# The first attention of a two-block layer rebuilt: one table set, the mask as an identity product, sums from a split softplus

## The chip, the core and the metric

The kernel runs on one core of one Trainium2 chip. A core has five engines with instruction streams of their own: TensorE (matrix products, PE in the profile, its weight loads PEld), VectorE (DVE), ScalarE (ACT), GpSimd (POOL) and SyncE (SP, which issues the transfers here). They share the memory SBUF; TensorE writes its results to PSUM, 8 banks of 128 x 512 fp32. They wait for each other by semaphores. The metric is the device time of one execution in microseconds.

## What is computed

Two blocks work on a sequence of 512 tokens and 1024 channels. The first has stick-breaking attention beside a state-space scan, the second RWKV-7, a sparse attention and two feed-forward parts. All is fp32. The change concerns the stick-breaking attention alone, 16 heads of 64 channels:

```python
z = einsum("bqhd,bkhd->bhqk", q, k) * scale
mask = s_idx < t_idx                                  # key before query
log_beta = log_sigmoid(z)
log_one_minus = where(mask, log_sigmoid(-z), 0.0)
tail = cumsum(log_one_minus, axis=3, reverse=True) - log_one_minus
weights = exp(where(mask, log_beta + tail, -inf))
out = einsum("bhqk,bkhd->bqhd", weights, v)
```

With softplus(z) = log(1 + exp(z)) the exponent is z minus the sum of softplus(z) over the keys from s up to t.

## The kernel before

The program is a chain of stages with a barrier between them; in each stage every engine has its own list of instructions, written out by hand, and the semaphores order them. No scheduler moves anything. The attention stage comes after the projections of q, k and v and ahead of a normalization (norm_sb). No transfer is issued in it: the weights of the next stages are already in a ring in SBUF.

One head is handled at a time, keys on the 128 partitions, queries along the columns. Of the 4 x 4 blocks of 128 x 128 only the 10 on and over the diagonal are kept: key block i has 512, 384, 256 and 128 columns, 1280 together, in three banks. There are two such areas in PSUM: zb (the scores) and wb (the exponent). For a head, before:

- TensorE makes the scores into zb (`scores`, L564).
- VectorE clamps them to 80 (L608) into SBUF; ScalarE takes exp (L631) and ln(1 + ...) (L633); VectorE takes the maximum with the scores in zb (L612). That is softplus. GpSimd multiplies the diagonal blocks by a mask (L650).
- TensorE makes the scores once more into wb (L588) and adds the sums over softplus with two constant matrices (L591), 10 matmuls in fp32.
- VectorE clamps wb to 0 and adds the constant `late`, which hides later keys (L620); ScalarE takes exp (L639); TensorE multiplies with v (`products`, L573), two heads into one bank; ScalarE copies each finished bank out (L627).

exp and ln lie in different table sets of ScalarE in this program, so a table load stands before each change. TensorE's order in turn hh is: sums(hh), scores of head hh + 2, products(hh - 1).

Of the kernel before, what the change touches and what calls it, by code (L numbers as in the profile page):

```python
# [13 lines left out]
P = 128  # L14
T = 512
D = 1024
KT = D // P
NB = T // P
HD = 64
H = D // HD  # L20
# [15 lines left out]
SB_W = [T - P * i for i in range(NB)]  # L36
SB_AT = [0, 512, 1024, 896]
SB_N = 1280
# [61 lines left out]
def program(nc, A, out, stop=None, dump=None):  # L100
    f32 = mybir.dt.float32
    ALU = mybir.AluOpType
    ACT = mybir.ActivationFunctionType
# [9 lines left out]
    def sem(name):  # L113

        section.append(nc.alloc_semaphore(name))
        return section[-1]
# [7 lines left out]
    with ctx:  # L124
        F = [sb(f"act{i}", [P, KT, T]) for i in range(5)]
# [10 lines left out]
        def give_up(first):  # L136

            while above and above[-1][0] >= first:
                above.pop()[1].close()

        def open_above(key, name, shape, dtype):
            one = ExitStack()
            above.append((key, one))
            return one.enter_context(nc.sbuf_tensor(name, shape, dtype))

        def restore(name):

            give_up(9)
            for i in range(5 + len(above), 9):
                F[i:] = [open_above(i, f"{name}_act{i}", [P, KT, T], f32)]  # L150
# [8 lines left out]
        late = sb("late", [P, SB_N])  # L159
        aux = sb("aux", [P, 3584])  # L160
# [6 lines left out]
        def mat(name):  # L167
            return squares[:, MAT_AT[name] * P:MAT_AT[name] * P + P]
# [307 lines left out]
        with nc.Block() as block:  # L476
            @block.scalar
            def _(act):
                nc.scalar.activation(small[:, 0:8], cols[:, COL_AT["c"]:COL_AT["c"] + 8], ACT.Silu).then_inc(c_ready, 1)  # L479
# [62 lines left out]
        checkpoint("v", v[:, :, :])  # L542


        o = F[5]
        work = F[6][:, :, :].rearrange("p a b -> p (a b)")
        clamped = [work[:, 0:SB_N], work[:, SB_N:2 * SB_N]]
        sp_m = [F[7][:, :, :].rearrange("p a b -> p (a b)")[:, i * SB_N:(i + 1) * SB_N] for i in range(2)]
        wts = [F[8][:, :, :].rearrange("p a b -> p (a b)")[:, i * SB_N:(i + 1) * SB_N] for i in range(2)]
        zb = PS[:, 0:3, :].rearrange("p a b -> p (a b)")  # L550
        wb = PS[:, 3:6, :].rearrange("p a b -> p (a b)")
        z_ready, z_taken, sp_step = sem("z_ready"), sem("z_taken"), sem("softplus_step")
        clamp_ready, log_ready, sp_ready = sem("clamp_ready"), sem("log_ready"), sem("sp_ready")
        w_ready, w_clamped, wts_ready = sem("w_ready"), sem("w_clamped"), sem("wts_ready")
        o_ready, o_taken, exp_done, late_masked = sem("o_ready"), sem("o_taken"), sem("sb_exp_done"), sem("sp_masked")
        with nc.Block() as block:
            def head(t, hh, a, b):
                return t[hh % 2 * HD:(hh % 2 + 1) * HD, hh // 2, a:b]

            @block.tensor  # L560
            def _(pe):
                def scores(hh, dst, stop):
                    for i in range(NB):
                        mm = nc.tensor.matmul(dst[:, SB_AT[i]:SB_AT[i] + SB_W[i]], head(k_, hh, i * P, (i + 1) * P),  # L564
                                              head(q, hh, i * P, T), start=True, stop=stop)
                    return mm

                def products(hh):
                    pe.wait_ge(wts_ready, hh + 1)
                    if hh >= 4 and hh % 2 == 0:  # L570
                        pe.wait_ge(o_taken, (hh - 4) // 2 + 1)
                    for i in range(NB):
                        mm = nc.tensor.matmul(PS[hh % 2 * HD:(hh % 2 + 1) * HD, 6 + hh // 2 % 2, i * P:T],  # L573
                                              v_tok[:, i, hh * HD:(hh + 1) * HD], wts[hh % 2][:, SB_AT[i]:SB_AT[i] + SB_W[i]],
                                              start=i == 0, stop=i == NB - 1)
                    mm.then_inc(o_ready, 1)


                scores(0, zb, True).then_inc(z_ready, 1)
                pe.wait_ge(sp_ready, 1)  # L580
                scores(1, zb, True).then_inc(z_ready, 1)
                for hh in range(H):
                    pe.wait_ge(late_masked, hh + 1)
                    if hh >= 1:
                        pe.wait_ge(w_clamped, hh)
                    for i in range(NB):

                        nc.tensor.matmul(wb[:, SB_AT[i]:SB_AT[i] + SB_W[i]], head(k_, hh, i * P, (i + 1) * P),  # L588
                                         head(q, hh, i * P, T), start=True, stop=False)
                        for j in range(i, NB):  # L590
                            mm = nc.tensor.matmul(wb[:, SB_AT[i] + (j - i) * P:SB_AT[i] + SB_W[i]],  # L591
                                                  mat("neg_ge" if i == j else "neg_ones"),
                                                  sp_m[hh % 2][:, SB_AT[j]:SB_AT[j] + SB_W[j]], start=False, stop=j == NB - 1)
                    mm.then_inc(w_ready, 1)
                    if hh + 2 < H:
                        pe.wait_ge(sp_ready, hh + 2)
                        scores(hh + 2, zb, True).then_inc(z_ready, 1)
                    if hh >= 1:
                        products(hh - 1)
                products(H - 1)  # L600

            @block.vector
            def _(dve):
                def softplus(hh):
                    dve.wait_ge(z_ready, hh + 1)
                    if hh >= 2:
                        dve.wait_ge(sp_ready, hh - 1)
                    nc.vector.tensor_scalar(clamped[hh % 2], zb[:, 0:SB_N], 80.0, None, ALU.min).then_inc(clamp_ready, 1)  # L608
                    dve.wait_ge(log_ready, hh + 1)
                    if hh >= 2:  # L610
                        dve.wait_ge(w_ready, hh - 1)
                    nc.vector.tensor_tensor(sp_m[hh % 2], clamped[hh % 2], zb[:, 0:SB_N], ALU.max).then_inc(sp_ready, 1)  # L612
                softplus(0)
                for hh in range(H):
                    if hh + 1 < H:
                        softplus(hh + 1)
                    dve.wait_ge(w_ready, hh + 1)
                    if hh >= 2:
                        dve.wait_ge(o_ready, hh - 1)
                    nc.vector.scalar_tensor_tensor(out=wts[hh % 2], in0=wb[:, 0:SB_N], scalar=0.0, in1=late[:, :],  # L620
                                                   op0=ALU.min, op1=ALU.add).then_inc(w_clamped, 1)

            @block.scalar
            def _(act):
                def out_pair(p):
                    act.wait_ge(o_ready, 2 * p + 2)
                    nc.scalar.copy(o[:, p, :], PS[:, 6 + p % 2, :]).then_inc(o_taken, 1)  # L627

                def logs(hh):
                    act.wait_ge(clamp_ready, hh + 1)  # L630
                    nc.scalar.activation(clamped[hh % 2], clamped[hh % 2], ACT.Exp).then_inc(exp_done, 1)  # L631
                    act.wait_ge(exp_done, hh + 1)
                    nc.scalar.activation(clamped[hh % 2], clamped[hh % 2], ACT.Ln, bias=1.0).then_inc(log_ready, 1)  # L633
                logs(0)
                for hh in range(H):
                    if hh + 1 < H:
                        logs(hh + 1)
                    act.wait_ge(w_clamped, hh + 1)
                    nc.scalar.activation(wts[hh % 2], wts[hh % 2], ACT.Exp).then_inc(wts_ready, 1)  # L639
                    if hh % 2 == 0 and hh >= 2:  # L640
                        out_pair(hh // 2 - 1)
                out_pair(H // 2 - 1)

            @block.gpsimd
            def _(pool):
                for hh in range(H):
                    pool.wait_ge(sp_ready, hh + 1)
                    for a, n in ((0, 1), (512, 1), (896, 2)):
                        part = sp_m[hh % 2][:, a:a + n * P].rearrange("p (n c) -> p n c", c=P)
                        last = nc.gpsimd.tensor_tensor(part, part, mat("lt").unsqueeze(1).to_broadcast([P, n, P]), ALU.mult)  # L650
                    last.then_inc(late_masked, 1)
        checkpoint("o", o[:, :, :])

        def conv_program(name, n_tiles, rhs, taps, w_col, b_col, dst, pair_out=None, split=None):
# [1079 lines left out]
```

## Time and profile before

| | |
|---|---|
| median of 3 runs | 3232.93 us (3232.72 to 3234.16) |
| span of the profiled execution | 3230.6 us (the profile gives no other time of it) |
| TensorE busy in the span | 2798.7 us, 87% |
| attention stage | 287.5 to 501.0 us, 213.5 us |
| busy in it: TensorE, ScalarE, VectorE, GpSimd | 205.28, 107.25, 71.51, 24.75 us |

The span is from the first to the last instruction. The stage's busy times come from the view that adds up the busy time of each engine in a stretch. Times in the timelines count from the start of the span. In them a row can stand for several instructions of one engine and line ("x8"): an fp32 matmul is recorded as two, one for each pass. Matmuls overlap at their ends, so the time from the start of one row to the start of the next is the better measure of their cost.

### The profile page before, as it was taken

To read this page: it belongs to the slowest core of one execution; us is meant where nothing else is said; L and a number is where in the kernel's file an instruction comes from. 1 tells how busy PE (TensorE), PEld (TensorE's weight loads), DVE (VectorE), ACT (ScalarE), POOL (GpSimd) and SP (SyncE) were. 2 spreads that over 40 slices of the span, in tenths; PEclk is the share of its full clock that TensorE was granted. 3 is DMA by queue.
4 is the path that set the end of the run, shared out by engine and by line. 5 is a ranking of instruction groups with operands and counts; after the bars stand their busy time and mean duration, and the time that the engine had idled before them with its cause. 6 is when DMAs were issued, how large, how long until landed. Compare 5 with 4: busy or idle time off the path is not lost. (4 is left out here: it accounts for less than half of the span.)

```text
span 3230.6 us, 31387 instructions
## 1 busy us (share of the span) xinstructions
PE 2798.7 (87%) x13080; PEld 2116.0 (65%) x13080; DVE 1350.8 (42%) x1997; ACT 736.1 (23%) x1043; POOL 84.9 (3%) x100
## 2 busy tenths in 40 slices
PE   7899999878988862999999698999986398899997
PEld 7777555666446722888888356887852155688786
DVE  0221331565114337554444335665312733466633
ACT  0232551223003321000000113222212144322222
POOL 0000110000000000001000000000000000000000
PEclk9999998978888975999899698999977699899998
DMA  5221001201112200000000011322203000122221
GB/s 198 76 85 46 1 1 39 69 25 46 52 59 68 82 17 0 1 1 1 1 1 1 10 61 50 98 95 87 92 10 116 0 1 5 48 98 98 92 92 39
DMA packets 45244, 158.57 MB, mean 49 GB/s; under 512 B 5056, under 2 KB 6976, under 8 KB 44720
## 3 DMA queue, kind: packets, MB, share of 16 engines
q1 hardware_dynamic: 43440, 149.71, 14.7%
q10 hardware_dynamic: 1664, 6.86, 0.6%
q8 instruction: 104, 1.70, 0.2%
q14 instruction: 36, 0.29, 0.0%
HBM read 154.41 MB, written 2.14 MB: 48 GB/s over the span
## 5 line engine op out<-in xcount | busy, mean ns | idle before, releaser
L694 PE MATMUL banks<-up_x_high,up_w_high 128*128 128x512 f32 x704 | 275.7, 392 | 20.4 <-DVE up_x_low L707 20.4
L695 PE MATMUL banks<-up_x_low,up_w_high 128*128 128x512 f32 x704 | 275.3, 391 | 0.0
L696 PE MATMUL banks<-up_x_high,up_w_low 128*128 128x512 f32 x704 | 275.2, 391 | 0.0
L264 PE MATMUL banks<-act,weight_ring 128*128 128x512 f32 (+1 forms) x528 | 236.9, 611 | 17.0 <-DVE act L948 12.6
L264 PEld LDWEIGHTS banks<-act,weight_ring 128*128 128x128 f32 (+1 forms) x528 | 102.2, 194 | 155.0 <-issue 152.5
L694 PEld LDWEIGHTS banks<-up_x_high,up_w_high 128*128 128x128 f32 x704 | 133.2, 189 | 51.1 <-issue 23.5
L677 DVE TENSOR_TENSOR up_w_low<-weight_ring,up_w_high 128x1024 fp32r<-128x1024 f32 x88 | 107.7, 1225 | 138.9 <-ACT up_w_high L672 138.9
L715 DVE SCALAR_TENSOR_TENSOR act<-banks,cols,act 128x511 f32<-128x511 f32 (+2 forms) x212 | 158.8, 749 | 7.5
L695 PEld LDWEIGHTS banks<-up_x_low,up_w_high 128*128 128x128 f32 x704 | 133.1, 189 | 27.9
L696 PEld LDWEIGHTS banks<-up_x_high,up_w_low 128*128 128x128 f32 x704 | 133.0, 189 | 27.8
L309 PE MATMUL banks<-down_x_high,down_w_high 128*128 128x512 f32 x352 | 139.3, 396 | 13.1 <-DVE down_x_low L348 13.1
L310 PE MATMUL banks<-down_x_low,down_w_high 128*128 128x512 f32 x352 | 138.7, 394 | 0.0
L311 PE MATMUL banks<-down_x_high,down_w_low 128*128 128x512 f32 x352 | 138.6, 394 | 0.0
L672 ACT CAST up_w_high<-weight_ring 128x1024 fp32r<-128x1024 f32 x88 | 92.1, 1049 | 191.3 <-PE banks L696 186.9
L346 DVE TENSOR_TENSOR down_w_low<-weight_ring,down_w_high 128x1024 fp32r<-128x1024 f32 x44 | 53.9, 1225 | 155.4 <-ACT down_w_high L330 155.4
L1158 PE MATMUL banks<-late,stat 128*128 128x128 f32 x768 | 106.8, 290 | 13.7 <-POOL v_act L1296 13.7
L1257 DVE TENSOR_TENSOR late<-banks,late 128x512 f32<-128x512 f32 x80 | 55.3, 691 | 148.0 <-PE banks L1173 148.0
L1170 PE MATMUL banks<-v_act,aux 128*128 128x128 f32 x768 | 111.8, 294 | 0.5
L1158 PEld LDWEIGHTS banks<-late,stat 128*128 128x128 f32 x768 | 96.9, 198 | 19.2 <-POOL v_act L1296 15.1
L1170 PEld LDWEIGHTS banks<-v_act,aux 128*128 128x128 f32 x768 | 101.0, 206 | 4.6 <-DVE aux L1245 3.0
L487 PE MATMUL banks<-small,weight_ring 128*128 128x1 f32 x384 | 82.1, 352 | 20.7 <-ACT small L479 20.7
L384 PE MATMUL banks<-squares,act 128*128 128x1 f32 x384 | 84.1, 342 | 13.7 <-ACT act L394 12.6
(367 smaller groups left out, 5134.1 us busy)
## 6 DMA issues: line engine op xcount, KB each, us to landing
weight_ring<-in_up SPq DMA_DIRECT2D x88, 512.0 KB, 3.4
weight_ring<-in_down SPq DMA_DIRECT2D x44, 512.0 KB, 3.4
weight_ring<-in_w_in SPq DMA_DIRECT2D x28, 512.0 KB, 3.6
weight_ring<-in_w_ada SPq DMA_DIRECT2D x24, 512.0 KB, 3.6
weight_ring<-in_w_rkv SPq DMA_DIRECT2D x24, 512.0 KB, 3.5
weight_ring<-in_w_out SPq DMA_DIRECT2D x16, 512.0 KB, 3.6
weight_ring<-in_w_q SPq DMA_DIRECT2D x8, 512.0 KB, 3.5
weight_ring<-in_w_k SPq DMA_DIRECT2D x8, 512.0 KB, 3.6
```

Of the source, the lines that this page charges most:

```text
L264: mm = nc.tensor.matmul(PS[0:n_cols, n % 4, :], w[:, k % 8 * n_cols:(k % 8 + 1) * n_cols], rhs(k), start=k == 0, stop=k == k_tiles - 1)
L309: nc.tensor.matmul(PS[:, n, :], high, x_high[:, k % 2, :], start=k == 0, stop=False)
L310: nc.tensor.matmul(PS[:, n, :], high, x_low[:, k % 2, :], start=False, stop=False)
L311: mm = nc.tensor.matmul(PS[:, n, :], low, x_high[:, k % 2, :], start=False, stop=last)
L672: nc.scalar.copy(w_high[:, n % 2, :], ring[:, i % RING, :]).then_inc(wh_made, 1)
L677: nc.vector.tensor_tensor(w_low[:, n % 2, :], ring[:, i % RING, :], w_high[:, n % 2, :].bitcast(f32), ALU.subtract).then_inc(wl_made, 1)
L694: nc.tensor.matmul(PS[:, n % 4, :], high, x_high[:, k, :], start=k == 0, stop=False)
L695: nc.tensor.matmul(PS[:, n % 4, :], high, x_low[:, k, :], start=False, stop=False)
L696: mm = nc.tensor.matmul(PS[:, n % 4, :], low, x_high[:, k, :], start=False, stop=k == 7)
L715: nc.vector.scalar_tensor_tensor(out=dst(n)[:, j:], in0=PS[:, n % 4, 0:T - j], scalar=w_col(n, taps - 1 - j), in1=dst(n)[:, j:], op0=ALU.m ...
L1158: mm = nc.tensor.matmul(PS[:, g, j * P:(j + 1) * P], four(N_, g)[:, j, :], four(GT, g)[:, j, :], start=True, stop=True)
L1170: mm = nc.tensor.matmul(PS[:, 2 + g, j * P:(j + 1) * P], four(Q, g)[:, j, :], four(G, g)[:, j, :], start=True, stop=True)
```

## The change

All in the attention stage, where n counts turns and `turns` gives the head of a turn (0, 2, 1, 3, 4, 6, 5, 7, ...):

- ScalarE first loads one table set that holds exp, ln and copy. It copies each head's scores out of zb into SBUF (`take_z`, zs, three buffers); the softplus works from there.
- Later keys are hidden on TensorE: a product of the identity with the constant block `late` adds -1e30 to the diagonal blocks of zb and wb (`hide_late`). GpSimd has no work left, and the clamp of wb to 0 is now a clamp of the exp to 1, in SBUF.
- Softplus is split on VectorE in a high part rounded to fp32r and the rest (`sp_high`, `sp_low`); the sums are 20 matmuls in fp32r instead of 10 in fp32. The constant matrices are converted to fp32r at the stage's start.
- TensorE alternates, score by score, between the head of turn n + 3 into zb and that of turn n + 1 into wb; one lies in partitions 0 to 63, the other in 64 to 127.
- The output o takes the place of q.

```diff
-                scores(0, zb, True).then_inc(z_ready, 1)
-                pe.wait_ge(sp_ready, 1)
-                scores(1, zb, True).then_inc(z_ready, 1)
-                for hh in range(H):
-                    pe.wait_ge(late_masked, hh + 1)
-                    if hh >= 1:
-                        pe.wait_ge(w_clamped, hh)
...
+                def score(hh, dst, i):
+
+                    nc.tensor.matmul(dst[:, SB_AT[i]:SB_AT[i] + SB_W[i]], head(k_, hh, i * P, (i + 1) * P),
+                                     head(q, hh, i * P, T), start=i < 3, stop=False, skip_group_check=True)
+
+                def hide_late(dst):
                     for i in range(NB):
+                        mm = nc.tensor.matmul(dst[:, SB_AT[i]:SB_AT[i] + P], ident_r, late_r, start=False, stop=False, skip_group_check=True)
                     return mm
...
+                def products(n):
+                    hh = turns[n]
+                    pe.wait_ge(wts_ready, n + 1)
+                    if n >= 4 and n % 4 < 2:
+                        pe.wait_ge(o_taken, hh // 2 - 1)
...
+                def sums(n):
+                    pe.wait_ge(low_ready, n + 1)
+                    for part in (sp_high, sp_low):
+                        for i in range(NB):
+                            for j in range(i, NB):
+                                mm = nc.tensor.matmul(wb[:, SB_AT[i] + (j - i) * P:SB_AT[i] + SB_W[i]], neg_ge_r if i == j else neg_ones_r,
+                                                      part[:, n % 2, SB_AT[j]:SB_AT[j] + SB_W[j]], start=False, stop=False, skip_group_check=True)
+                    mm.then_inc(w_ready, 1)
+
+                pe.wait_ge(mats_ready, 4)
+                for n in range(3):
+                    if n:
+                        pe.wait_ge(z_copied, n)
                     for i in range(NB):
...
+                        score(turns[n], zb, i)
+                    hide_late(zb).then_inc(z_ready, 1)
+                for i in range(NB):
+                    score(turns[0], wb, i)
+                hide_late(wb)
+                for n in range(H):
+                    sums(n)
+                    if n >= 1:
+                        products(n - 1)
+                    if n + 3 < H:
+                        pe.wait_ge(z_copied, n + 3)
+                    if n + 1 < H:
+                        pe.wait_ge(w_exped, n + 1)
+                    for i in range(NB):
+                        if n + 3 < H:
+                            score(turns[n + 3], zb, i)
+                        if n + 1 < H:
+                            score(turns[n + 1], wb, i)
+                    if n + 3 < H:
+                        hide_late(zb).then_inc(z_ready, 1)
+                    if n + 1 < H:
+                        hide_late(wb)
                 products(H - 1)
 
             @block.vector
             def _(dve):
...
+                def clamp(n):
+                    dve.wait_ge(z_copied, n + 1)
+                    if n >= 3:
+                        dve.wait_ge(low_ready, n - 2)
+                    nc.vector.tensor_scalar(soft[n % 3], zs[n % 3], 80.0, None, ALU.min).then_inc(clamped, 1)
+
+                def softplus(n):
+                    dve.wait_ge(logged, n + 1)
+                    nc.vector.tensor_tensor(soft[n % 3], soft[n % 3], zs[n % 3], ALU.max).then_inc(soft_ready, 1)
+                    dve.wait_ge(soft_ready, n + 1)
+                    if n >= 2:
+                        dve.wait_ge(w_ready, n - 1)
+                    nc.vector.tensor_copy(sp_high[:, n % 2, :], soft[n % 3]).then_inc(high_ready, 1)
+                    dve.wait_ge(high_ready, n + 1)
+                    nc.vector.tensor_tensor(sp_low[:, n % 2, :], soft[n % 3], sp_high[:, n % 2, :].bitcast(f32), ALU.subtract).then_inc(low_ready, 1)
...
+                clamp(0)
                 softplus(0)
...
+                clamp(1)
+                softplus(1)
+                clamp(2)
+                for n in range(H):
+                    if n + 2 < H:
+                        softplus(n + 2)
+                    dve.wait_ge(w_exped, n + 1)
+                    nc.vector.tensor_scalar(wts[n % 2], wts[n % 2], 1.0, None, ALU.min).then_inc(wts_ready, 1)
+                    if n + 3 < H:
+                        clamp(n + 3)
...
+                def take_z(n):
+                    act.wait_ge(z_ready, n + 1)
+                    if n >= 3:
+                        act.wait_ge(soft_ready, n - 2)
+                    nc.scalar.copy(zs[n % 3], zb[:, 0:SB_N]).then_inc(z_copied, 1)
+
+                def logs(n):
+                    act.wait_ge(clamped, n + 1)
+                    nc.scalar.activation(soft[n % 3], soft[n % 3], ACT.Exp).then_inc(exped, 1)
+                    act.wait_ge(exped, n + 1)
+                    nc.scalar.activation(soft[n % 3], soft[n % 3], ACT.Ln, bias=1.0).then_inc(logged, 1)
+
+                nc.scalar.preload_act_table_set("natural_log_exp_and_others")
+                take_z(0)
                 logs(0)
...
+                take_z(1)
+                logs(1)
+                take_z(2)
+                for n in range(H):
+                    act.wait_ge(w_ready, n + 1)
+                    if n >= 2:
+                        act.wait_ge(o_ready, n - 1)
+                    nc.scalar.activation(wts[n % 2], wb[:, 0:SB_N], ACT.Exp).then_inc(w_exped, 1)
+                    if n + 3 < H:
+                        take_z(n + 3)
+                    if n + 2 < H:
+                        logs(n + 2)
+                    if n >= 3 and (n - 1) % 4 >= 2:
+                        out_pair(2 * ((n - 1) // 4) + (n - 1) % 4 - 2)
                 out_pair(H // 2 - 1)
...
```

On ScalarE, one turn in the middle of the stage before (k_act holds softplus and the weights, first_act the clamped scores, banks is PSUM):

```order
L631 ACTIVATE first_act<-first_act 128x1280 [waits clamp_ready]
L633 ACT_TABLE_LOAD
L633 ACTIVATE first_act<-first_act 128x1280 [waits sb_exp_done]
L639 ACT_TABLE_LOAD
L639 ACTIVATE k_act<-k_act 128x1280 [waits w_clamped]
```

and one turn of the same engine now (aux holds the weights; L687 is the exp of the weights, L669 take_z, L673 and L675 the two steps of logs):

```order
L687 ACTIVATE aux<-banks 128x1280 [waits o_ready,w_ready]
L669 COPY first_act<-banks 128x1280 [waits sb_soft_ready,sb_z_ready]
L673 ACTIVATE first_act<-first_act 128x1280 [waits sb_clamped]
L675 ACTIVATE first_act<-first_act 128x1280 [waits sb_exp_done]
L663 COPY act<-banks 128x512 [waits o_ready]
```

The table loads are gone, and a copy that waits for TensorE's scores stands ahead of the exp and ln of the head before. On VectorE, one turn before:

```order
L608 TENSOR_SCALAR first_act<-banks 128x1280 [waits sp_ready,z_ready]
L612 TENSOR_TENSOR k_act<-first_act,banks 128x1280 [waits w_ready,log_ready]
L620 SCALAR_TENSOR_TENSOR k_act<-banks,late 128x1280 [waits o_ready,w_ready]
```

and now (L634 is the maximum of softplus(n+2), L638 and L640 its high and low part, L655 the clamp of the weights of turn n, L630 the clamp of the scores of turn n + 3):

```order
L634 TENSOR_TENSOR first_act<-first_act 128x1280 [waits sb_log_done]
L638 CAST sb_sp_high<-first_act 128x1280 [waits w_ready,sb_soft_ready]
L640 TENSOR_TENSOR sb_sp_low<-first_act,sb_sp_high 128x1280 [waits sb_high_ready]
L655 TENSOR_SCALAR aux<-aux 128x1280 [waits w_exped]
L630 TENSOR_SCALAR first_act<-first_act 128x1280 [waits sb_low_ready,sb_z_copied]
```

Three operations have become five, and no longer read PSUM. On TensorE now, from the products of turn n - 1 to the first sums of turn n + 1 (L581 products, L567 scores, L572 the mask, L591 sums; sb_mats holds the converted constants):

```order
L581 MATMUL banks<-aux,act 64x512 [waits wts_ready]
L581 MATMUL banks<-aux,act 64x384
L581 MATMUL banks<-aux,act 64x256
L581 MATMUL banks<-aux,act 64x128
L567 MATMUL banks<-act 128x512 [waits w_exped,sb_z_copied]
L567 MATMUL banks<-act 128x512
L567 MATMUL banks<-act 128x384 x2
L567 MATMUL banks<-act 128x256 x2
L567 MATMUL banks<-act 128x128 x2
L572 MATMUL banks<-sb_mats 128x128 x8
L591 MATMUL banks<-sb_sp_high,sb_mats 128x512 [waits sb_low_ready]
```

The products stood behind the scores of a later head and now stand ahead of them; the second set of scores has moved from between the sums to beside those.

## Rows read from the trace of the kernel before

**Rows 1.** By stretch: length, PE, PEld, DVE, ACT, POOL busy, clock; groups of table loads.

```profile
287.50:290.10 2.60, 2.39 (x8) 1.40 (x8) 0.15 (x1) 1.26 (x1) 0.00 (x0) 1.00 0.65 208
290.10:303.80 13.70, 6.90 (x12) 3.43 (x13) 4.32 (x3) 5.81 (x5) 1.54 (x3) 0.50 0.00 0
303.80:501.00 197.20, 195.99 (x685) 109.34 (x683) 67.04 (x45) 100.17 (x84) 23.21 (x45) 1.00 0.00 1
sum 213.50, PE 205.28 PEld 114.18 DVE 71.51 ACT 107.25 POOL 24.75; mean PE 68.43 PEld 38.06 DVE 23.84 ACT 35.75 POOL 8.25
...
L633 ACT ACT_TABLE_LOAD x16 | 20.5, 1283 | 0.3
L639 ACT ACT_TABLE_LOAD x15 | 19.2, 1283 | 0.3
```

**Rows 2.** Timelines over one head: start, us, engine, line, operation, [idle <- releaser].

```profile
319.65 2.42 PE L564 MATMUL banks<-act 64*128 64x512 f32 x8
322.00 2.37 PE L573 MATMUL banks<-k_act,act 128*64 128x512 f32 x8
324.30 1.12 PE L588 MATMUL banks<-act 64*128 64x512 f32 x2
...
332.35 2.42 PE L564 MATMUL banks<-act 64*128 64x512 f32 x8
...
327.52 1.49 DVE L612 TENSOR_TENSOR k_act<-first_act,banks 128x1280 f32<-128x1280 f32 x1 [3.92 <-ACT first_act L633]
```

**Rows 3.** Fp32r matmuls of 512 columns by stretch; timeline of the v projection's end.

```profile
200.00:229.00 29.00, 28.26 (x125) 23.08 (x123) 7.31 (x8) 10.95 (x16) 0.00 (x0) 1.00 0.29 90
...
283.75 2.84 PE L525 MATMUL banks<-weight_ring,act 128*128 128x128 f32 x24
```

**Rows 4.** Timelines of TensorE: two heads' scores, and the scan's alternating halves.

```profile
300.05 1.22 PE L588 MATMUL banks<-act 64*128 64x512 f32 x1
300.47 0.84 PE L564 MATMUL banks<-act 64*128 64x256 f32 x2
...
693.28 0.44 PE L908 MATMUL banks<-after_conv_act 128*64 128x128 f32 x4
693.50 0.44 PE L909 MATMUL banks<-after_conv_act 128*64 128x128 f32 x4
```

**Rows 5.** Groups by shape (count, busy us, mean ns), and timeline rows of handovers.

```profile
L1643 ACT COPY aux<-banks 128x1280 f32<-128x1280 f32 x16 | 19.6, 1225 | 75.9 <-PE banks L1563 75.9
L633 ACT ACTIVATE first_act<-first_act 128x1280 f32<-128x1280 f32 x16 | 20.3, 1269 | 0.2
L859 DVE TENSOR_TENSOR after_conv_act<-after_conv_act 128x1024 f32<-128x1024 f32 x4 | 4.9, 1226 | 0.4
L1514 DVE TENSOR_SCALAR act<-act 128x512 f32<-128x512 f32 x1 | 0.4, 419 | 0.0
L1514 DVE TENSOR_SCALAR act<-act 128x256 f32<-128x256 f32 x1 | 0.3, 293 | 0.0
...
322.11 1.49 DVE L608 TENSOR_SCALAR first_act<-banks 128x1280 f32<-128x1280 f32 x1 [0.86 <-PE banks L564]
323.63 1.27 ACT L631 ACTIVATE first_act<-first_act 128x1280 f32<-128x1280 f32 x1 [1.08 <-DVE first_act L608]
...
496.68 1.27 ACT L639 ACTIVATE k_act<-k_act 128x1280 f32<-128x1280 f32 x1 [8.60 <-DVE k_act L620]
498.01 2.37 PE L573 MATMUL banks<-k_act,act 128*64 128x512 f32 x8 [0.59 <-ACT k_act L639]
```

**Rows 6.** The clock by stretch after pauses of TensorE, with the pauses in its timeline.

```profile
703.20:713.40 10.20, 6.64 (x61) 6.45 (x62) 9.96 (x18) 4.67 (x9) 0.00 (x0) 0.83 0.00 1
...
710.21 0.70 PE L908 MATMUL banks<-after_conv_act 128*64 128x128 f32 x4 [3.56 <-DVE after_conv_act L872]
...
1078.60:1085.40 6.80, 5.97 (x14) 4.75 (x15) 3.74 (x6) 0.53 (x2) 0.00 (x0) 0.50 0.00 0
...
1079.43 0.76 PE L309 MATMUL banks<-v_x_high,v_w_high 128*128 128x512 f32 x1 [4.21 <-DVE v_x_low L348]
```

More of the change, by code:

```diff
@@ L542, in program @@
         checkpoint("v", v[:, :, :])
[L545 to L549, printed above, removed]
+        o = F[2]
+        give_up(7)
+        sp_high, sp_low, mats_r = (open_above(9, "sb_" + n, shape, mybir.dt.float32r) for n, shape in
+                                   (("sp_high", [P, 2, SB_N]), ("sp_low", [P, 2, SB_N]), ("mats", [P, 4 * P])))
+        third = lambda t, i: t[:, :, :].rearrange("p a b -> p (a b)")[:, i * SB_N:(i + 1) * SB_N]
+        zs, soft, wts = [third(F[5], i) for i in range(3)], [third(F[6], i) for i in range(3)], [aux[:, 0:SB_N], aux[:, SB_N:2 * SB_N]]
+        turns = [4 * (i // 4) + (0, 2, 1, 3)[i % 4] for i in range(H)]
+        neg_ge_r, neg_ones_r, ident_r, late_r = (mats_r[:, i * P:(i + 1) * P] for i in range(4))
         zb = PS[:, 0:3, :].rearrange("p a b -> p (a b)")
         wb = PS[:, 3:6, :].rearrange("p a b -> p (a b)")
[L552 to L555, printed above, removed]
+        z_ready, z_copied, clamped, exped, logged = (sem("sb_" + n) for n in ("z_ready", "z_copied", "clamped", "exp_done", "log_done"))
+        soft_ready, high_ready, low_ready = sem("sb_soft_ready"), sem("sb_high_ready"), sem("sb_low_ready")
+        w_ready, w_exped, wts_ready = sem("w_ready"), sem("w_exped"), sem("wts_ready")
+        o_ready, o_taken, mats_ready = sem("o_ready"), sem("o_taken"), sem("sb_mats_ready")
         with nc.Block() as block:
@@ L561, in _ @@
             def _(pe):
-                def scores(hh, dst, stop):
+                def score(hh, dst, i):
+                    nc.tensor.matmul(dst[:, SB_AT[i]:SB_AT[i] + SB_W[i]], head(k_, hh, i * P, (i + 1) * P),
+                                     head(q, hh, i * P, T), start=i < 3, stop=False, skip_group_check=True)
+                def hide_late(dst):
                     for i in range(NB):
-                        mm = nc.tensor.matmul(dst[:, SB_AT[i]:SB_AT[i] + SB_W[i]], head(k_, hh, i * P, (i + 1) * P),
-                                              head(q, hh, i * P, T), start=True, stop=stop)
-                    return mm
@@ L568, in products @@
[L568 to L571, printed above, removed]
+                        mm = nc.tensor.matmul(dst[:, SB_AT[i]:SB_AT[i] + P], ident_r, late_r, start=False, stop=False, skip_group_check=True)
+                    return mm
+                def products(n):
[3 more added lines that the diff above has]
+                        pe.wait_ge(o_taken, hh // 2 - 1)
@@ L572, in products @@
                     for i in range(NB):
                         mm = nc.tensor.matmul(PS[hh % 2 * HD:(hh % 2 + 1) * HD, 6 + hh // 2 % 2, i * P:T],
-                                              v_tok[:, i, hh * HD:(hh + 1) * HD], wts[hh % 2][:, SB_AT[i]:SB_AT[i] + SB_W[i]],
+                                              v_tok[:, i, hh * HD:(hh + 1) * HD], wts[n % 2][:, SB_AT[i]:SB_AT[i] + SB_W[i]],
                                               start=i == 0, stop=i == NB - 1)
                     mm.then_inc(o_ready, 1)
-                scores(0, zb, True).then_inc(z_ready, 1)
@@ L580, in _ @@
-                pe.wait_ge(sp_ready, 1)
-                scores(1, zb, True).then_inc(z_ready, 1)
-                for hh in range(H):
-                    pe.wait_ge(late_masked, hh + 1)
-                    if hh >= 1:
-                        pe.wait_ge(w_clamped, hh)
-                    for i in range(NB):
[L588 to L599, printed above, removed]
+                def sums(n):
[6 more added lines that the diff above has]
+                    mm.then_inc(w_ready, 1)
@@ L603, in _ @@
             def _(dve):
[L604 to L612, printed above, removed]
@@ L613, in _ @@
-                softplus(0)
[L614 to L621, printed above, removed]
+                def clamp(n):
[3 more added lines that the diff above has]
+                    nc.vector.tensor_scalar(soft[n % 3], zs[n % 3], 80.0, None, ALU.min).then_inc(clamped, 1)
@@ new lines, in _ @@
+                nc.vector.tensor_copy(neg_ge_r, mat("neg_ge")).then_inc(mats_ready, 1)
+                nc.vector.tensor_copy(neg_ones_r, mat("neg_ones")).then_inc(mats_ready, 1)
+                nc.vector.tensor_copy(ident_r, mat("ident")).then_inc(mats_ready, 1)
+                nc.vector.tensor_copy(late_r, late[:, 0:P]).then_inc(mats_ready, 1)
+                clamp(0)
+                softplus(0)
+                clamp(1)
[8 more added lines that the diff above has]
+                        clamp(n + 3)
@@ L625, in out_pair @@
                 def out_pair(p):
-                    act.wait_ge(o_ready, 2 * p + 2)
+                    act.wait_ge(o_ready, 4 * (p // 2) + 3 + p % 2)
                     nc.scalar.copy(o[:, p, :], PS[:, 6 + p % 2, :]).then_inc(o_taken, 1)
[L629 to L633, printed above, removed]
@@ L634, in _ @@
-                logs(0)
[L635 to L641, printed above, removed]
-                out_pair(H // 2 - 1)
[L644 to L651, printed above, removed]
+                def take_z(n):
[3 more added lines that the diff above has]
+                    nc.scalar.copy(zs[n % 3], zb[:, 0:SB_N]).then_inc(z_copied, 1)
@@ L652, in program @@
+                out_pair(H // 2 - 1)
+        restore("after_sb")
         checkpoint("o", o[:, :, :])
```

## The prediction

> **What bounds the kernel now.** I read the page's slices first, then the busy time of each engine in the stretch of the first attention, then the timelines of TensorE, ScalarE and VectorE over one head. The stage runs from 287.5 to 501.0 us [rows 1], 213.5 us of a 3230.6 us span; the change touches nothing outside it. Within it TensorE is busy 205.28 us, ScalarE 107.25, VectorE 71.51, GpSimd 24.75. From 303.8 on TensorE is busy 195.99 of 197.20 us at the full clock [rows 1], so there the stage is bound by TensorE. One head takes it from 319.65 to 332.35 [rows 2], 12.70 us: 2.35 for the scores of a later head, 2.30 for the products with v, 8.05 for the second set of scores and the sums over softplus (10 matmuls, in fp32 each two passes). The waits of the other engines cost nothing there: VectorE's 3.92 us before L612 [rows 2] and ScalarE's table loads lie beside TensorE's work. Only the ends are exposed: 290.1 to 303.8 has the lower clock and 6.90 us of work in 13.70.
>
> **What goes and what TensorE then has to do.** The 31 table loads inside the heads (1.28 us each [rows 1]), the reads of PSUM by VectorE and GpSimd's masking go. All of them are hidden, so they give nothing by themselves. TensorE's work for a head becomes:
> - Sums: 20 one-pass matmuls in fp32r in place of 10 two-pass ones. One of 512 columns costs 28.26/125 = 0.226 us [rows 3]; one of 128 columns about 0.11 (the v projection's 24 in 2.84 us [rows 3]). Interpolating 0.17 and 0.12 for 384 and 256 columns: 2 x (0.226 + 2 x 0.17 + 3 x 0.12 + 4 x 0.11) = 2.7, with a changeover 2.9 us.
> - Products: unchanged, 2.30.
> - Both sets of scores, alternating between a head in the lower and one in the upper 64 rows. In the only place where before has such neighbours, they run at once: L588's first matmul starts at 300.05 and L564's next at 300.47 [rows 4], and the scan's matmuls on alternating halves of the columns come four in 0.22 us, at half the 0.11 each of rows 3. I take 2.35 for both sets, once rather than twice. The upper bound is 4.65.
> - The mask by the identity: 4 matmuls of 128 columns per bank set, 0.45 to 0.5 us, twice.
>
> The sum is 2.9 + 2.3 + 2.35 + 1.0 + 0.3 for changeovers = 8.9 us against 12.70. If TensorE still set the pace, the stage would lose some 45 us. It doesn't, as I read the new order.
>
> **The wait that takes over.** In ScalarE's new order the copy of a head's scores out of PSUM (take_z(n+3), L669) stands ahead of the exp and ln of the head before it (logs(n+2)). It waits for scores that TensorE makes only after products(n-1). In VectorE's new order the clamp of the weights of head n (L655) stands behind softplus(n+2), which waits for that ln. And products(n), in TensorE's next turn, waits for that clamp. So every turn is one closed chain: products, scores of a later head, mask, copy, exp, ln, max, high part, low part, clamp, next products. Before, the clamp of the weights also stood behind the softplus of a later head, but the scores of that head had been made a turn earlier, so the chain had a turn's slack. Queued behind L655 stands clamp(n+3), which nobody needs yet; behind take_z stand only the logs; sums(n+1) runs beside the chain.
>
> The chain, each piece from a row:
> - TensorE: 2.30 products + 2.35 scores + 0.5 mask + 0.2 until the last matmul has ended = 5.35.
> - ScalarE: copy of 1280 columns from PSUM 1.225 (the second attention's L1643 [rows 5]), exp 1.27 and ln 1.27 (L633 has 1269 ns), three handovers of 0.04 (L608 ends at 323.60, L631 starts at 323.63): 3.89 [rows 5].
> - VectorE: max 1.49 (1226 ns for 1024 columns in SBUF [rows 5], L612's 1.49 for 1280 [rows 2]), low part 1.49 the same. High part and clamp read one tile in SBUF and write to SBUF. The nearest rows are L1514's [rows 5]: 293 and 419 ns at 256 and 512 columns, 0.49 ns a column, so 0.80 at 1280. The upper bound for each is L608's 1.49, from PSUM. Taken: 1.49 + 0.80 + 1.49 + 0.80 + 0.12 for handovers = 4.70.
> - Back to TensorE: 0.06 (L639 ends 497.95, L573 starts 498.01 [rows 5]).
>
> That makes 14.0 us for a turn at full clock, against 12.70, and TensorE idle 14.0 - 8.9 = 5 us in each, in one piece between the sums and the products.
>
> For the cast to fp32r no row has VectorE's time. The Trainium skill, "VectorE: DVE Perf Modes", "What auto-detection actually checks", says that an operation with one source takes a double-rate mode when source and destination are both in SBUF; L1514 agrees with it. By it the cast is at the 0.80 that I take; without it the stage would be 12 x 0.69 = 8 us longer.
>
> **The clock.** A repeated idle piece of that size has neighbours in this trace. In the scan, TensorE is idle 3.56 us ahead of 710.21, and the 10.2 us turn before that has a granted clock of 0.83 [rows 6] (the five others of the same view read 0.83 too), which is 3.4 us at 1.2 GHz. Before the v projection of the second block it is idle 4.21 us, and then 6.8 us go at 0.50, although it is busy 5.97 of them [rows 6]. After a gap the lower level covers the first few us of work, and here these are on the chain: the products and scores. 3.4 us at half rate cost 1.7, 6.8 us cost 3.4; at the stage's start 6.90 us of work, half of it on 64 rows, ran at 0.50 before the clock rose [rows 1]. So the short one alone is not enough, and I take the middle, 2.55. A turn is then 16.55 us. The bounds are 14.0 (never low) and 19.35 (all 5.35 us doubled).
>
> The Trainium skill, "TensorE: Matmul & The Clock Gate", "HAM oscillation — how this bites in real kernels", has this as a rule against such loops: one that waits between bursts of matmuls starts each burst at the lower clock. Rows 6 agree with it; without it the forecast would be 12 x 2.55 = 31 us less.
>
> **Start and end of the stage.** Start: four conversions of 128 columns on VectorE (about 0.9), then three heads' scores, each of which now waits until ScalarE has copied the one before. From 287.5: scores and mask 288.4 to 292.3 (the lower clock from 290.1, as before), copy to 293.7, second scores at half rate 2 x 2.8 to 299.4, copy to 300.9, softplus(0) to 301.0, clamp and logs(1) to 304.4, third scores to 306.6, the scores and sums of head 0 to 314.9 (5.85 us of work, the first 4.9 us at half rate), exp 316.3, scores of the fourth head 319.4, copy, exp, ln 323.2, VectorE's 4.7 to 327.9. I take 327 for the first products, where before has 322.00 [rows 2]; at full clock it would be 324. From there 12 turns bring products(12). Then the tail, in which no scores of later heads are made: logs, softplus and clamp until products(13) 8.2, its products and the last scores and sums 8.1, products(14) 2.3, products(15) and the last copy 3.1; 21.7 at full clock, 24 with the first stretch at half.
>
> **The sum.** Stage end = 327 + 12 x 16.55 + 24 = 549.6, against 501.0: 48.6 us later. The profile gives no time but its span of 3230.6; the median of the runs is 3232.93, 2.3 above, which I leave as it is: 3232.9 + 48.6 = 3281.5. Nothing after the stage uses what has moved: DMA is idle in it, the weights ahead are in the ring, and norm_sb works on another tile of the same size. GpSimd's absence is worth 0.
>
> **Rivals.**
> - *The chain at nearly full clock.* The gaps of 5 us pass without a drop, or it passes before the products start. Turns of 14.0 to 15.2: 324 + 12 x 14.0 + 22 = 514, to 324 + 182 + 23 = 529; time 3246 to 3261. For it: 287.5 to 290.1, right after a change of stage, is at 1.00 [rows 1]. Against: rows 6. 0.12.
> - *More than I take.* The two sets of scores don't run side by side (+2.3), or the cast or clamp runs at 1.49 (+0.69 each), or all of the chain's matmuls are at half rate: turns of 18 to 19.4, end at 327 + 216 + 25 = 568 to 585, time 3300 to 3317. For it: alternation inside a head's scores isn't in the trace, only its edge. 0.15.
> - *Faster: TensorE goes on setting the pace.* The place is TensorE's wait before L581: if the clamped weights are there in time, the turn is TensorE's own 8.9 us. The whole comes out faster below a chain of (501 - 324 - 22)/12 = 12.9 us at full clock. At 8.9 the stage ends at 324 + 107 + 22 = 453, the time is 3185. Against: ScalarE and VectorE alone have 3.89 + 4.70 on it. 0.04.
> - *No difference.* The same sum with a chain of 12.4 to 13.4, for which both short operations and the scores must be shorter than any row. 0.04.
>
> **Numbers.** The forecast (turns of 15 to 18) has 0.65 and 3263 to 3299 as its own range. To hold 8 in 10 the range takes in most of the chain at full clock and part of the longer case: 3250 to 3308. About 0.2%, 6.5 us, is what a measurement can tell from none; slower by more than that are the first two rivals and the forecast, 0.92.
>
> **What would show it.** In the profile after: TensorE's idle time in the stage is before L581, released by VectorE's L655, about 5 us each; products follow each other at 16 to 17 us; VectorE waits before L634 for ScalarE's L675; the granted clock of the stage is near 0.8 rather than 0.97; L567's matmuls of two heads start in pairs; L638 and L655 take 0.8 us. The stage ends near 550. I am wrong if products follow each other at under 13 us, or if TensorE's idle time is released by something other than L655.

## The result and the profile after

The changed kernel takes 3278.77 us (median of 4 runs, 3272.68 to 3280.44) against 3233.28 before: a ratio of 1.0137, 95% interval 1.0123 to 1.0151. It is 45.5 us slower, where 48.6 were forecast. The difference lies in the attention stage. The next stage's first work on ScalarE, norm_sb, starts at 547.98 instead of 501.29, 46.7 us later, and the span is 47.5 us longer.

By stretch (columns as in [rows 1]: length, then busy time of PE, PEld, DVE, ACT, POOL, the granted clock, DMA):

```profile
287.50:303.80 16.30, 13.03 (x29) 7.83 (x30) 5.96 (x9) 8.48 (x7) 0.00 (x0) 0.58 0.11 34
303.80:501.00 197.20, 138.46 (x637) 90.27 (x637) 62.67 (x59) 57.89 (x52) 0.00 (x0) 0.78 0.00 0
501.00:560.00 59.00, 46.78 (x219) 33.98 (x218) 16.83 (x17) 21.82 (x25) 0.00 (x0) 0.82 0.00 1
```

In the 197.20 us in which TensorE was busy 195.99 at full clock it is now busy 138.46, at a mean clock of 0.78. It waits for 58.7 us of them, and part of what it does runs slower. Who is waited for, from 330 to 525 us (engine and line that waits, what it waits for: us in total, times, longest):

```profile
ACT first_act L669 <- PE banks L572: 131.4, 12, 11.9
DVE first_act L634 <- ACT first_act L675: 127.6, 12, 11.4
...
PE banks L581 <- DVE aux L655: 67.8, 13, 5.2
```

These three are the chain's three handovers between engines: TensorE's masked scores to the copy, the ln to the softplus, the clamp of the weights to the products. TensorE has no other idle time of note. One turn, on the three engines (start, us, engine, line, operation):

```profile
413.33 3.79 PE L581 MATMUL banks<-aux,act 128*64 128x512 f32 x8 [5.22 <-DVE aux L655]
417.06 2.43 PE L567 MATMUL banks<-act 64*128 64x512 f32 x16
419.41 1.11 PE L572 MATMUL banks<-sb_mats 128*128 128x128 f32 x8
420.36 1.55 PE L591 MATMUL banks<-sb_sp_high,sb_mats 128*128 128x512 f32 x10
421.75 1.56 PE L591 MATMUL banks<-sb_sp_low,sb_mats 128*128 128x512 f32 x10
428.52 4.53 PE L581 MATMUL banks<-aux,act 128*64 128x512 f32 x8 [5.22 <-DVE aux L655]
...
420.11 1.23 ACT L669 COPY first_act<-banks 128x1280 f32<-128x1280 f32 x1 [10.36 <-PE banks L572]
421.24 1.27 ACT L673 ACTIVATE first_act<-first_act 128x1280 f32<-128x1280 f32 x1
422.54 1.27 ACT L675 ACTIVATE first_act<-first_act 128x1280 f32<-128x1280 f32 x1
...
423.85 1.49 DVE L634 TENSOR_TENSOR first_act<-first_act 128x1280 f32<-128x1280 f32 x1 [9.83 <-ACT first_act L675]
425.37 0.83 DVE L638 CAST sb_sp_high<-first_act 128x1280 fp32r<-128x1280 f32 x1
426.23 1.49 DVE L640 TENSOR_TENSOR sb_sp_low<-first_act,sb_sp_high 128x1280 fp32r<-128x1280 f32 x1
427.64 0.82 DVE L655 TENSOR_SCALAR aux<-aux 128x1280 f32<-128x1280 f32 x1
```

Read it as a closed path: products 413.33 to 417.06, scores to 419.41, the mask until the copy starts at 420.11, copy, exp and ln until 423.85, VectorE until the next products at 428.52. The parts are 3.73 + 2.35 + 0.70 + 3.74 + 4.67 = 15.19 us. The sums run beside the copy and are done 5.22 us before the weights are. The products take 3.73 here and 4.46 in the next turn, where [rows 2] have 2.30: they run partly at 1.2 GHz. Turns of about 16.1, 16.6 and 15.2 us follow each other, and in the short ones it is the products that take 3.7 us rather than 4.5. The first products start at 332.32, those of turn 12 at 524.10, so 12 turns take 191.8 us, 15.98 each, against 12.70 before.

### The profile page after: what moved, and what is told of

It reads as the page before. It is cut to its first block and busy times, and to the rows that moved or that the text cites. A ratio compares the mean times of both kernels' runs of the same rounds, so it can differ in the third digit from the quotient of the medians.

```text
span 3278.1 us, 31625 instructions
## 1 busy us (share of the span) xinstructions
PE 2781.5 (85%) x13208; PEld 2124.2 (65%) x13208; DVE 1365.5 (42%) x2033; ACT 712.3 (22%) x1027; POOL 60.2 (2%) x52
## 3 DMA queue, kind: packets, MB, share of 16 engines
HBM read 154.41 MB, written 2.14 MB: 48 GB/s over the span
## 5 line engine op out<-in xcount | busy, mean ns | idle before, releaser
L581 PE MATMUL banks<-aux,act 128*64 128x512 f32 (+3 forms) x128 | 63.0, 662 | 67.8 <-DVE aux L655 67.8
L1202 PE MATMUL banks<-late,stat 128*128 128x128 f32 x768 | 106.5, 289 | 13.8 <-POOL v_act L1340 13.8
```

The lines of the kernel that those rows point to most:

```text
L1202: mm = nc.tensor.matmul(PS[:, g, j * P:(j + 1) * P], four(N_, g)[:, j, :], four(GT, g)[:, j, :], start=True, stop=True)
```

## The experiments

Nine kernels were run. All times are medians; each was compared with the kernel before on its own chip (3231.2 to 3233.6 us).

**The weights' clamp ahead of the softplus** (e1_clamp_first). On VectorE:

```diff
                 for n in range(H):
-                    if n + 2 < H:
-                        softplus(n + 2)
                     dve.wait_ge(w_exped, n + 1)
                     nc.vector.tensor_scalar(wts[n % 2], wts[n % 2], 1.0, None, ALU.min).then_inc(wts_ready, 1)
+                    if n + 2 < H:
+                        softplus(n + 2)
                     if n + 3 < H:
                         clamp(n + 3)
```

> Only VectorE's order in a turn changes: the clamp of the weights of turn n comes ahead of softplus(n+2), not behind it. Theory (a closed chain of one turn through products, scores, copy, exp, ln, softplus, weights' clamp): the chain is opened, TensorE's idle 5.2 us ahead of the products go, the clock stays at 1.00 in the middle of the stage, a turn falls from 16.0 to TensorE's own 8.6 to 9 us, and the time to about 3278 - 12 x 7 = 3194 (3185 to 3210), below the kernel before. Rival (the operations added on VectorE and ScalarE are themselves the pace): their sum per turn stays, so 3270 to 3280.

Measured: 3179.59 us, ratio 0.9839 (0.9824 to 0.9854). Two statements exchanged take 99 us off the changed kernel and put it 54 below the kernel before. TensorE's timeline over a turn, and its busy time and clock from 340 to 420 us:

```profile
391.74 2.37 PE L581 MATMUL banks<-aux,act 128*64 128x512 f32 x8
394.09 2.43 PE L567 MATMUL banks<-act 64*128 64x512 f32 x16
396.45 1.11 PE L572 MATMUL banks<-sb_mats 128*128 128x128 f32 x8
397.39 1.55 PE L591 MATMUL banks<-sb_sp_high,sb_mats 128*128 128x512 f32 x10
398.78 1.54 PE L591 MATMUL banks<-sb_sp_low,sb_mats 128*128 128x512 f32 x10
400.25 2.37 PE L581 MATMUL banks<-aux,act 128*64 128x512 f32 x8
...
340.00:420.00 80.00, 80.00 (x486) 58.02 (x486) 49.71 (x47) 48.09 (x44) 0.00 (x0) 1.00 0.00 1
```

There is no idle time left, and a turn is TensorE's own work: 2.35 + 2.36 + 0.94 + 2.86 = 8.51 us. The rival, that the added work on VectorE and ScalarE sets the pace, has fallen: they do the same work in 80 us for more heads and are busy 49.71 and 48.09.

**The logs ahead of the copy** (e2_logs_first). VectorE as in the changed kernel; on ScalarE `logs(n + 2)` stands before `take_z(n + 3)`.

> Only ScalarE's order in a turn changes: exp and ln of turn n+2 come ahead of the copy of the scores of turn n+3. Theory: the chain is cut at another place; the weights' clamp still stands behind softplus(n+2), but that no longer waits for scores made in the same turn. From the end of sums(n): exp 1.25, logs 2.55, softplus 3.85, clamp 0.82 = 8.5 us until products(n) may start, beside TensorE's 8.5 us for products, scores, mask and sums: a turn of 8.6 to 9.5, time 3190 to 3215. Rival (it is VectorE's order alone that matters): as the changed kernel, 3270 to 3280.

Measured: 3178.13 us, ratio 0.9834 (0.9817 to 0.985). The turn is 8.49 us as well. So it is not one engine's order that is wrong, but the chain that both close together, and cutting it at either place is enough. The time was below the range expected in both experiments: 8.5 us a turn was right, but I had left the start of the stage as it was, and the first products came at 323.9 instead of 332.3.

**TensorE kept busy on the closed chain** (e3_filler). The chain stays; ahead of the wait for the weights, with FILL = 5:

```diff
                     hh = turns[n]
-                    pe.wait_ge(wts_ready, n + 1)
                     if n >= 4 and n % 4 < 2:
                         pe.wait_ge(o_taken, hh // 2 - 1)
+                    for _ in range(FILL if n < H - 3 else 0):
+                        nc.tensor.matmul(PS[hh % 2 * HD:(hh % 2 + 1) * HD, 6 + hh // 2 % 2, :],
+                                         mat("neg_ones")[:, 0:HD], squares[:, 0:T], start=True, stop=True)
+                    pe.wait_ge(wts_ready, n + 1)
```

> The chain is left as it is; ahead of the wait for the weights TensorE runs 5 two-pass fp32 matmuls of 512 columns (about 0.85 us each) into the bank that the products overwrite, so it is not idle there. Theory (the lower clock after each pause costs 1.5 to 2.8 us of the turn, on the chain): the clock is 1.00 from the middle of the stage on, a turn takes 13.8 to 14.1 us, time 3278 - 12 x 2 = about 3254 (3248 to 3260). Rival (the clock falls beside the chain and costs nothing): 3275 to 3285.

Measured: 3250.85 us, ratio 1.0056 (1.0041 to 1.0071): useless work makes the changed kernel 27.9 us faster. A turn:

```profile
401.97 2.37 PE L585 MATMUL banks<-aux,act 128*64 128x512 f32 x8 [0.78 <-DVE aux L659]
404.27 2.43 PE L568 MATMUL banks<-act 64*128 64x512 f32 x16
406.63 1.11 PE L573 MATMUL banks<-sb_mats 128*128 128x128 f32 x8
407.57 1.55 PE L595 MATMUL banks<-sb_sp_high,sb_mats 128*128 128x512 f32 x10
408.96 1.56 PE L595 MATMUL banks<-sb_sp_low,sb_mats 128*128 128x512 f32 x10
410.45 4.50 PE L581 MATMUL banks<-squares 128*64 128x512 f32 x10
415.73 1.72 PE L585 MATMUL banks<-aux,act 128*64 128x512 f32 x4 [0.78 <-DVE aux L659]
...
340.00:420.00 80.00, 75.28 (x353) 42.14 (x354) 31.71 (x30) 28.28 (x25) 0.00 (x0) 1.00 0.00 1
```

The clock stays at 1.00 and the turn is 13.76 us, the chain at full clock. The difference from 15.98 is 2.22 us, in 12 turns 26.6 us: nearly all of the 27.9. This kernel splits the loss: at full clock the changed kernel is 17 us slower than the kernel before, and the clock that falls in its pauses costs the other 28.

**Both sets of scores on the same rows** (e4_same_rows: `turns = list(range(H))`, and the wait for a free output bank at each even n from 4 on). Once on the closed chain, and once with the clamp moved (e5_same_rows_open).

> The heads are taken in their plain order, so that the two alternating sets of scores lie in the same 64 rows of the array. Theory (sets in different rows run at once, 2.35 us for both): they now take 4.5 us at full and up to 9 at half clock, on the chain: +2.2 to +4.4 us a turn, time 3305 to 3325. Rival (the pairing is worth nothing, or is hidden): 3273 to 3285.

> The kernel of e1_clamp_first (clamp of the weights ahead of softplus), with the heads in plain order, so that the two alternating sets of scores share the same 64 rows. Theory (once the chain is open TensorE is the pace, and the pairing saves it a whole set of scores): a turn goes from 8.5 to 10.6, the time to 3179.6 + 13 x 2.15 = 3207 (3202 to 3213). Rival (the pairing mattered only on the chain): 3178 to 3183.

Measured: 3315.12 us (ratio 1.0256, 1.0241 to 1.0271) and 3214.63 us (0.9947, 0.9932 to 0.9962). In e4 a turn is 18.47 us against 15.98. The sixteen recorded score matmuls in e5:

```profile
400.00 4.58 PE L567 MATMUL banks<-act 64*128 64x512 f32 x16
404.51 1.11 PE L572 MATMUL banks<-sb_mats 128*128 128x128 f32 x8
```

4.51 us to the next group, where alternating rows have 2.36. Its turn is 10.63 us against 8.49, and 12 x 2.14 = 25.7 of the 35 us are that. The other 10 come ahead of the first products (333.9 against 323.9), and I had not expected them. The two sets that follow the first sums take 8.87 us there, on one half of the rows and at 1.2 GHz, and the clock comes back only at 334 instead of 316. The timeline's row, and the stretch (with the busy times and the clock):

```profile
318.10 8.87 PE L567 MATMUL banks<-act 64*128 64x512 f32 x16 [1.42 <-ACT aux L687]
...
290.00:334.00 44.00, 39.95 (x109) 28.38 (x108) 12.94 (x12) 13.65 (x11) 0.00 (x0) 0.50 0.00 0
```

**The start of the stage** (e6_start_paired, e7_start_filled). Both start from e1. Heads in the order 0, 1, 3, 2, with the copies of the output banks and the waits for them changed to suit, and, in the loop over the first three score sets:

```diff
                     for i in range(NB):
                         score(turns[n], zb, i)
+                        if n == 1:
+                            score(turns[0], wb, i)
                     hide_late(zb).then_inc(z_ready, 1)
-                for i in range(NB):
-                    score(turns[0], wb, i)
-                hide_late(wb)
+                    if n == 1:
+                        hide_late(wb)
```

> e1_clamp_first with the heads in the order 0, 1, 3, 2, which lets the second scores of head 0 run beside the scores of turn 1 at the start, not after those of turn 2; one set of scores less in a row while the clock is low (4.6 us). Theory (at the start the order on TensorE is the path): 3179.6 - 4.5 = 3175 (3173 to 3177). Rival (ScalarE's and VectorE's softplus of head 0 and 1 is the path there): 3178 to 3181.

> e6_start_paired with two-pass fp32 matmuls on the whole array (128 x 128, 512 columns) in TensorE's pauses at the start: one ahead of the first scores, two ahead of each wait for a copied set. They write to a bank that is overwritten later. Theory (the long stretch at 1.2 GHz at the stage's start comes from pauses and scores on 64 rows alone, and full-array work between them brings the clock back sooner): the first products come 6 to 12 us earlier, 3163 to 3170. Rival (the clock doesn't come back sooner): the fillers only delay, 3175 to 3182.

Measured: 3169.67 us (0.9809, 0.9794 to 0.9823) and 3166.78 (0.98, 0.9785 to 0.9815); the two intervals overlap. e7 is the best version: 64 us or 2.0% below the kernel before. The pairing brought more than the 4.5 us expected: e6's first products start at 316.06 instead of 323.87, and since its profile enters the stage 0.9 us later, the stage is 8.7 us shorter than in e1. (The medians are 9.9 us apart, but stand on two chips on which the kernel before differs by 2.4.) What was not expected is the clock: in e1 it is at 1.2 GHz from 289 to 316 without a break, in e6 it is back at 307.2 for the rest of the stage (length, busy times, clock):

```profile
297.00:300.40 3.40, 2.53 (x18) 1.81 (x15) 3.33 (x3) 1.23 (x1) 0.00 (x0) 1.00 0.00 0
300.40:307.20 6.80, 6.80 (x23) 5.50 (x22) 4.09 (x5) 3.77 (x3) 0.00 (x0) 0.50 0.00 0
307.20:316.00 8.80, 7.38 (x54) 6.44 (x52) 2.31 (x3) 4.24 (x4) 0.00 (x0) 1.00 0.00 0
```

In e7's profile the first products start at 313.02, 3.0 us ahead of e6's 316.06, and 0.75 us of that lies ahead of the stage; 6 to 12 were expected. The start of e7:

```profile
286.81 1.10 PE L597 MATMUL banks<-squares 128*128 128x512 f32 x2 [0.93 <-PEq L516]
287.83 2.42 PE L567 MATMUL banks<-act 64*128 64x512 f32 x8
...
305.23 3.81 PE L567 MATMUL banks<-act 64*128 64x512 f32 x16 [1.73 <-ACT aux L694]
```

The scores at 287.83 run at full clock throughout, and only those at 305.23, after a pause of 1.73 us, take 3.75 us instead of 2.35. Ahead of them lies a path through ScalarE and VectorE on which no clock of TensorE bears: from the first copy at 290.88 to the end of the first weights' exp at 305.09 the two engines hand over to each other without a gap (first copy, clamp, exp, ln, softplus, the second head's clamp, exp and ln, the third copy, the exp).

**The sums without the split** (e8_plain_sums). e1 with 10 fp32 matmuls over the unsplit softplus, and without the cast and the subtraction:

```diff
-                    nc.vector.tensor_tensor(soft[n % 3], soft[n % 3], zs[n % 3], ALU.max).then_inc(soft_ready, 1)
-                    dve.wait_ge(soft_ready, n + 1)
                     if n >= 2:
                         dve.wait_ge(w_ready, n - 1)
...
+                    nc.vector.tensor_tensor(sp_plain[:, n % 2, :], soft[n % 3], zs[n % 3], ALU.max).then_inc(low_ready, 1)
```

> e1_clamp_first without the split: the sums are 10 two-pass fp32 matmuls over the unsplit softplus, and VectorE has no high and low part to make. Theory (TensorE is the pace): the sums take 4.32 us instead of 2.8, a turn 10.0, the time 3179.6 + 16 x 1.5 = 3204 (3199 to 3209). Rival (the two VectorE operations cost as much as the split gives): 3175 to 3185.

Measured: 3206.13 us (0.9922, 0.9905 to 0.9938). The sums:

```profile
403.28 4.55 PE L592 MATMUL banks<-sb_sp_unused,squares 128*128 128x512 f32 x20
407.75 2.37 PE L582 MATMUL banks<-aux,act 128*64 128x512 f32 x8
```

4.47 us for one head against 2.86 in e1, a turn of 10.08 against 8.49. The split is worth about 26 us once TensorE is the pace (25.8 in the length of the stage, 26.5 between the medians).

**The table loads alone** (e9_before_one_table). The kernel before with one line more, `nc.scalar.preload_act_table_set("natural_log_exp_and_others")` at the stage's start.

> The kernel before with one edit: the table set that holds exp and ln is loaded once at the stage's start, so that the 31 loads inside the heads (1.28 us each, 40 us together) are gone and nothing else changes. Theory (they lie beside TensorE's work, all but one in the first softplus): 0 to 2.6 us less, 3230 to 3233. Rival (ScalarE's loads lengthen the turn): up to 40 us less, about 3195.

Measured: 3231.04 us (median of 11 runs), ratio 0.9995 (0.9986 to 1.0004): no difference that the runs can tell. In the profile the stage is 0.7 us shorter. ScalarE is busy 60.81 us from 303.8 to 501.0 instead of 100.17, TensorE as before:

```profile
303.80:501.00 197.20, 195.14 (x683) 108.81 (x681) 67.12 (x46) 60.81 (x55) 23.22 (x45) 1.00 0.00 0
```

40 us less work on an engine that isn't the bound are worth next to nothing.

## Why the prediction was right

- *The chain.* It was read from the order of the instructions, and e1 and e2 show it by cutting it at two different places, each with the same result. Its length at full clock was forecast as 14.0 us and is 13.76 in e3. Scores side by side 2.35 (2.35 measured), mask and end of the last matmul 0.70 (0.70), ScalarE 3.89 (3.74, successive instructions overlap by up to 0.1), VectorE and the way back 4.76 (4.67).
- *The durations that no row had.* The cast to fp32r takes 826 ns and the clamp 820 where 0.80 was taken; the upper bound of 1.49 was far off. The rule of the Trainium skill, "VectorE: DVE Perf Modes", "What auto-detection actually checks", on the double-rate mode held for a cast to fp32r as well.
- *TensorE's work.* 8.9 us forecast for a turn, 8.49 measured. The sums' interpolated 2.7 to 2.9 is 2.86, the rest is the 0.3 put down for changeovers, which did not show.
- *The clock.* 2.55 us a turn forecast, 2.22 measured by e3 against the changed kernel. The forecast was the middle between a short and a long stretch at 1.2 GHz (1.7 and 3.4 us); against e3's 13.76 the turns cost 2.3, 2.8 and 1.4 us in a row, so the mean is near the middle because long and short ones mix. That mixture was not foreseen. (The stretch of 10.2 us in [rows 6] holds the pause of 3.56 us and the work behind it, though the prediction calls it the turn before; its 0.83 stands.) The mean clock of the middle of the stage is 0.78, forecast near 0.8. The rule of the Trainium skill, "TensorE: Matmul & The Clock Gate", "HAM oscillation — how this bites in real kernels", on loops with pauses agrees with every turn of the trace: the products behind the pause take 3.7 to 4.5 us, where 2.30 are the full speed.
- *Start and tail.* The first products were put at 327 (the working there came to 327.9) and start at 332.3: the clock came back at 324.1, not near 311, so the first head's sums took 5.3 us and the paired scores behind them 4.56, where full speed is 2.86 and 2.35. The tail was put at 24 and is 23.6. The start's error of 5.3 us and that of the turns, 12 x (15.98 - 16.55) = -6.8, nearly cancel. So the forecast stage end of 549.6, with 547.7 measured, is closer than its terms: that the total is within 3.1 us is luck, the chain and its length are not.
- *The rivals.* The chain at nearly full clock would be e3, 3250.85. TensorE as the pace is e1, 3179.59, where 3185 was given. Scores on the same rows is e4, 3315.12 with a turn of 18.47, within the 3300 to 3317 and the 18 to 19.4 of that case. Each was a real alternative, one edit away.

What stays open is the start. e7 shows that work in TensorE's pauses keeps the clock up there, but its 2.9 us over e6 are within the intervals of the two. Why the clock stays low for so long in e1 and comes back early in e6 no run separates.

## What to carry to other kernels

When work is moved between engines, write down for one turn of the loop which instruction waits for which, and follow it in every engine's order until it comes back to where it began: the sum along such a circle is the least time of a turn, whatever the busiest engine has to do. Here two harmless-looking orders, a copy ahead of the logs and a clamp behind the softplus, made a circle of 13.8 us around TensorE's 8.5, and either exchange undid it. Count the clock too: here a wait of 5 us in each turn cost 2.2 us more through slower matmuls after it.

## What the runs showed of the hardware

- Two sets of 64-row matmuls in opposite halves of the array ran fully at once: 2.36 us for both, 4.51 when they shared a half (e1, e5), two passes each, alternating pair by pair.
- At the stage's start TensorE can be busy nearly all the time and stay at 1.2 GHz: 39.95 of 44.00 us in e5, 24.37 of the 27.00 from 289 in e1. The same came in the middle of the stage in e4, with scores on one half of the rows: busy 19.69 of the 20.50 us from 403.3, all at 1.2 GHz. With two sets of scores side by side earlier (e6) it was at 2.4 GHz from 297.0 to 300.4 and again from 307.2, and with full-array work in the pauses (e7) it fell only at 306.1, for 3.4 us. What in these differences decides is not settled by these runs.
- Idle time filled with useless matmuls made a kernel 28 us faster (e3): the clock stayed at 1.00, and the matmuls on the chain took 2.22 us less a turn.
